# Stores of the projection results moved from the scalar engine's queue to GpSimd's

## The reference, cut to what matters

```python
(z, xbc, dt_raw, gq, gk, gv, gr, glr, mq, mk, mv, mi, mf, mo, br) = jnp.split(h @ p['w_in'], idx, axis=-1)
...
y, ssd_new = _ssd_scan(xs * dt[..., None], dt * a, bm, cm, s0)
...
o, gla_new = _gla_scan(q, k, v, la.reshape(bsz, length, GLA_HEADS, GLA_DK), gla0.astype(f32))
...
hm, (mc_new, mn_new, mm_new) = _mlstm_scan(q, k, v, ig, lf, mc0.astype(f32), mn0.astype(f32), mm0.astype(f32))
...
merged = (g[:, :, 0] * (y_a @ p['w_br_ssd']) + g[:, :, 1] * (y_b @ p['w_br_gla'])
          + g[:, :, 2] * (y_c @ p['w_br_ml']))
return merged @ p['w_out'], (conv_new, ssd_new, gla_new, mc_new, mn_new, mm_new)
```

## Time and profile before

| | us |
|---|---|
| median of 3 runs | 1900.76 |
| the 3 runs | 1897.83, 1900.76, 1903.87 |
| the profiled execution, whole | 1900.96 |
| its span (first to last instruction) | 1899.2 |
| PE busy | 1755.5 (92%) |
| DVE busy | 882.7 (46%) |
| ACT busy | 580.6 (31%) |
| POOL busy | 108.1 (6%) |

### The profile page before, as it was taken

How to read it: one execution, slowest core, us unless ns; L and a number is a source line. 1 busy time by engine, 2 the same in 40 slices (tenths; PEclk the granted TensorE clock), 3 DMA queues, 4 the chain that set the end, 5 groups by cost and what they waited for, 6 DMA issues and landing times.

```text
span 1899.2 us, 30580 instructions
## 1 busy us (share of the span) xinstructions
PE 1755.5 (92%) x12284; PEld 1641.1 (86%) x12284; DVE 882.7 (46%) x1563; ACT 580.6 (31%) x1189; POOL 108.1 (6%) x154
## 2 busy tenths in 40 slices
PE   3499999999799999999999889999899999999994
PEld 0477898898699999889988779999899999999993
DVE  1455535545375555433433334465564444344444
ACT  1233423333333333233333334332342222222221
POOL 0000001210032121000000000000000000000001
PEclk7599999999899999999999999999999999999997
DMA  7665332356434343764444865444323322222211
GB/s 271 179 230 182 91 107 91 117 159 199 153 115 156 110 145 124 247 189 132 144 129 137 264 203 178 157 142 157 111 68 101 89 67 73 84 67 89 67 45 56
DMA packets 237349, 257.34 MB, mean 136 GB/s; under 512 B 14995, under 2 KB 220491, under 8 KB 234136
## 3 DMA queue, kind: packets, MB, share of 16 engines
q1 hardware_dynamic: 208984, 226.54, 37.7%
q10 hardware_dynamic: 28224, 28.85, 4.5%
HBM read 196.73 MB, written 58.62 MB: 134 GB/s over the span
## 4 chain that ended last, share of the span: by engine, by line
issue 43%; PE 41%; DMA 3%; DVE 3%; ACT 1%; DVEq 1%; POOLq 1%; POOL 1%; ACTq 0%; SPq 0%; PEldq 0%; PEld 0%
PE pj_acc L639 6%; PE pj_acc L640 6%; PE pj_acc L641 6%; PE pj_acc L646 5%; PE pj_acc L647 4%; PE pj_acc L648 4%; PE mx L1822 2%; DMA ar_w<-in_w_ada 1%; PE mx L2571 1%; PE mx L1319 1%; PE mx L1332 1%; DMA mg_y<-ys 1%; DVE pj_lo L609 0%; DVE ss_state L1180 0%; PE mx L1389 0%
## 5 line engine op out<-in xcount | busy, mean ns | idle before, releaser
L639 PE MATMUL pj_acc<-pj_act_hi,pj_lo 128*128 128x320 f32 x1808 | 575.5, 318 | 0.8 <-issue 0.7
L641 PE MATMUL pj_acc<-pj_act_hi,pj_hi 128*128 128x320 f32 x1808 | 560.1, 310 | 0.0
L640 PE MATMUL pj_acc<-pj_act_lo,pj_hi 128*128 128x320 f32 x1808 | 560.1, 310 | 0.0
L639 PEld LDWEIGHTS pj_acc<-pj_act_hi,pj_lo 128*128 128x128 f32 x1808 | 341.3, 189 | 22.1 <-issue 21.0
L640 PEld LDWEIGHTS pj_acc<-pj_act_lo,pj_hi 128*128 128x128 f32 x1808 | 341.4, 189 | 3.9 <-issue 2.9
L641 PEld LDWEIGHTS pj_acc<-pj_act_hi,pj_hi 128*128 128x128 f32 x1808 | 340.9, 189 | 0.0
L609 DVE TENSOR_TENSOR pj_lo<-pj_raw,pj_hi 128x1024 fp32r<-128x1024 f32 (+1 forms) x196 | 242.6, 1242 | 162.6 <-ACT pj_hi L602 159.7
L602 ACT ACTIVATE pj_hi<-pj_raw 128x1024 fp32r<-128x1024 f32 (+1 forms) x196 | 205.2, 1053 | 223.1 <-PE mx L2855 116.3
L646 PE MATMUL pj_acc<-pj_lo,pj_act_hi 128*128 128x256 f32 x880 | 259.4, 295 | 12.5 <-DVE pj_act_lo L2649 4.4
L647 PE MATMUL pj_acc<-pj_hi,pj_act_lo 128*128 128x256 f32 x880 | 252.6, 287 | 0.0
L648 PE MATMUL pj_acc<-pj_hi,pj_act_hi 128*128 128x256 f32 x880 | 252.2, 287 | 0.0
(11 more groups left out here) (359 smaller groups left out, 2130.9 us busy)
## 6 DMA issues: line engine op xcount, KB each, us to landing
pj_raw<-in_w_in SPq DMA_DIRECT2D x50, 1024.0 KB, 5.6
ar_w<-in_w_ada SPq DMA_DIRECT2D x16, 1024.0 KB, 5.7
pm<-pj_tm_out ACTq DMA_DIRECT2D x100, 128.0 KB, 2.1
pj_raw<-in_w_ffn_gate SPq DMA_DIRECT2D x22, 512.0 KB, 4.0
pj_raw<-in_w_ffn_up SPq DMA_DIRECT2D x22, 512.0 KB, 5.3
pj_raw<-in_w_ffn_down SPq DMA_DIRECT2D x11, 1024.0 KB, 5.0
ada_w<-in_w_ada SPq DMA_DIRECT2D x8, 1024.0 KB, 11.6
ml_c_b<-in_state_mlstm_c SPq DMA_DIRECT2D x32, 256.0 KB, 4.3
```

Source lines behind the costliest of these rows:

```text
L639: nc.tensor.matmul(out, lo[:, k, col], ahi[:, k, tok], start=(k == 0), stop=False)
L640: nc.tensor.matmul(out, hi[:, k, col], alo[:, k, tok], start=False, stop=False)
L641: last = nc.tensor.matmul(out, hi[:, k, col], ahi[:, k, tok], start=False, stop=(k == KT - 1))
```

## The change

The function that begins the store of unit u-2 keeps its place in the plan (the entry of unit u) but is called in POOL's walk of the list and no longer in ACT's. Its waits go with it: for the bank to be read out, and for mo also for the tanh. The rings, the data, the semaphores and the DMAs' shapes are unchanged. In the changed program the lines of the copies in `act_unit` have numbers lower by 2 (690 is 688), those behind the new function higher by 2 (729 is 731, 1281 is 1283).

```diff
             self.split_hi(act, k, q)
         if u >= 1:
             self.act_late(act, u - 1)
-        if u >= 2:
-            self.act_store(act, u - 2)
...
-    def act_store(self, act, u):
+    def pool_unit(self, pool, u):
+        if u >= 2:
+            self.pool_store(pool, u - 2)
+
+    def pool_store(self, pool, u):
         n, x = self.units[u]
         c, r = self.chunks[n], self.ring[u]
         if c.how in self.CM:
-            self.evicted(act, u)
+            self.evicted(pool, u)
             dst = self.pt if c.how == "copy_cm" else self.gt
             row = c.dst + (x // 2) * P
-            act.dma_start(dst[row:row + P, (x % 2) * HALF:(x % 2 + 1) * HALF], self.cm_out[:, r % self.RING, :]
+            pool.dma_start(dst[row:row + P, (x % 2) * HALF:(x % 2 + 1) * HALF], self.cm_out[:, r % self.RING, :]
                           ).then_inc(self.cm_stored[r % self.RING], 16)
         elif c.how in self.TM:
-            self.evicted(act, u)
+            self.evicted(pool, u)
             if c.how == "bias_tm":
-                act.wait_ge(self.biased, self.nth[u] + 1)
-            act.dma_start(self.pm[x * P:(x + 1) * P, c.dst:c.dst + CW], self.tm_out[:, r % self.RING, :]
+                pool.wait_ge(self.biased, self.nth[u] + 1)
+            pool.dma_start(self.pm[x * P:(x + 1) * P, c.dst:c.dst + CW], self.tm_out[:, r % self.RING, :]
                           ).then_inc(self.tm_stored[r % self.RING], 16)
...
         def _(pool):
             for stage, x in plan:
-                if stage is not None:
+                if stage is None:
+                    proj.pool_unit(pool, x)
+                else:
```

## The result

The changed kernel takes 1906.59 us (median of 20 runs), the kernel before 1900.07 (20 runs beside them). The ratio is 1.0035, with a 95% interval of 1.0025 to 1.0044: **slower by 6.5 us**, more than the 0.3% (5.7 us) within which the prediction called a change none. It had forecast 1900 and "same".

What follows compares the result with a forecast made beforehand. PE, busy 1755.5 of 1899.2 us, was taken as the bound, so only its waits count. 1900.96 - 1.0 (first SSD tile) + 0 (all else) = 1899.96, by the median 1899.8, stated as 1900; range 1895 to 1908.

Steps and rivals of the forecast that it cites:

- first SSD tile: POOL's products of SSD tile 0 start at about 256.3, 25 us later, behind 13 z stores: -1.0 us.
- mLSTM's start: POOL's clearing of 74 semaphores, which PE awaits: 0 at 1.0 us a store, +1.5 at 2.88.
- What is given to POOL: A POOL store costs between 0.33 and 2.88 us, taken as 1.0; 196 us in 944, for which POOL has room.
- Price of a DMA, ACT's side: 196 stores of 0.326 us leave ACT's sequencer: 0 booked; at most 9.4 us of PE's waits could go.
- PE's wait at 234.5: In the first SSD tile, without POOL's products beside DVE's `pj_lo`, down from 3.62 to about 2.6 us: gain 0.99.
- The configuration: POOL's configuration instruction moves into the first SSD tile: up to 6.9 us cost nothing; the skill page's 6 us leaves 0.9.
- Last SSD tile: A store ready at 388.86 waits behind `xd` until 403.50 and lands about 406.6, before the copy at 408.12: 0, at worst +3.
- a sign of error: The prediction is wrong if ACT or DVE wait for a store's landing near 269 us; no such ACT wait expected.
- GLA and the clearing: Stores ahead of POOL's 42 GLA arguments: 0, at worst +5; ahead of semaphore clearing before mLSTM: 0, at worst +1.5.
- DVE and POOL don't collide at stores: Judges the rival that POOL's stores stretch DVE's `pj_lo` at 12 weight chunks: +10.3 us, 1910; chance 0.12.
- The slower case: Slower by more than 0.3% (5.7 us): collisions of DVE and POOL 0.12, dear DMAs at several places 0.04; chance 0.16.

Runs made afterwards that it cites:

- e_late: Kernel before plus four more power operations inside the last root of mLSTM (32-byte tile): ratio 1.0032 to the kernel before.
- e_warm_a: Changed kernel plus a power operation on a constant ahead of each of 15 waits for squares, 512-byte tile: ratio 1.0011 to the kernel before.
- e_after2: The changed kernel again, on the same chip as the runs with the 512-byte tile: ratio 1.0031 to the kernel before.
- e_tiny_rest: Kernel before, stores on ACT, plus 176 small POOL DMAs, none between mLSTM's fourth and last root (32-byte tile): ratio 1.0017 to the kernel before.
- e_tiny2: Kernel before, stores on ACT, plus 196 small POOL DMAs to scratch memory, repeated (32-byte tile): ratio 1.0038 to the kernel before.
- e_tiny_p2: Kernel before, stores on ACT, plus only the 65 small POOL DMAs after the clearing ahead of mLSTM, large tile: ratio 1.0018 to the kernel before.
- e_tiny_p1: Kernel before, stores on ACT, plus only the 131 small POOL DMAs before the clearing ahead of mLSTM, large tile: ratio 1.0001 to the kernel before.
- e_cm_last: Only the cm_out stores on POOL, plus one power operation ahead of mLSTM's last root (32-byte tile): ratio 1.0032 to the kernel before.
- e_cm: Kernel before with only the 96 cm_out stores moved to POOL, those of tm_out left on ACT: ratio 1.0022 to the kernel before.
- e_tm: Kernel before with only the 100 tm_out stores moved to POOL, those of cm_out left on ACT: ratio 1.0014 to the kernel before.
- e_tiny_a: Kernel before, stores on ACT, plus 196 small POOL DMAs to scratch memory, 512-byte tile: ratio 1.0032 to the kernel before.
- e_first: Kernel before with POOL only waiting for the first 13 z results, no DMA, so its first SSD products come later: ratio 1.0000 to the kernel before.

## Why the prediction was wrong, step by step

**The step that failed** is the list of handovers, from "first SSD tile" to "mLSTM's start", which ends in "+ 0". With the price of a store from "What is given to POOL" it asked which copies, products, GLA arguments and clearings come later. It did not ask two things. First, mLSTM's roots were left out, though the view of PE's waits that it read has the row `mg_y<-ys`, 7.6 us, ahead of all but one other; "ends with a DMA" was taken for "not POOL's", where the DMA only ends a chain from ACT's squares over POOL's root and DVE to a store and a load. Second, the price of a DMA was sought in the DMA instruction alone. It is 0.54 us, cheaper than the 1.0 taken, and still POOL loses up to 5 us, at the operation behind it. No row of before had a DMA of POOL and a root side by side, so the term had no price there; what the rows could have told is the slack of each POOL result, and the last root's is zero (`e_late`: 4.6 us of root, 4.6 us of wait). The sum also has no term for the clock, which by the estimate above goes with 4.0 of the 6.5 us.

By ratios that place is worth about 0.2% (4 us) in three comparisons: `e_warm_a` against `e_after2`, `e_tiny_rest` against `e_tiny2`, `e_tiny_p2` against `e_tiny_p1`. By the means of the same runs they are 1.7, 3.2 and 3.2 us, each give or take 1.8 to 2.1, and only the second leaves out the last root's DMAs alone: the first repairs all 15 roots, the third has the DMAs of all five mLSTM roots. `e_late` speaks for less: less the tile it is 1.0021, 4 us for 4.6 us of wait, so that the 2.2 to 2.4 us of the changed kernel would cost about 2 us. **The size of this term is thus 2 to 4 us of the 6.5.** What it costs beyond its wait may be clock; that is my reading and not shown. One comparison speaks against: `e_cm_last`, less the tile, is 1.0021, as `e_cm` is, though its wait fell from 9.7 to 8.3; the intervals of both, 0.001 wide to each side, leave room for either. **Open** is the rest, a third to two thirds of the loss (`e_warm_a` 1.0011, `e_tm` 1.0014 with no store of POOL among mLSTM's later roots). The profiles show candidates, none tested alone: the 0.4 to 0.7 us of wait that go with real stores ahead of the merge, the clearing, and the waits in GLA.

**Price of a DMA, ACT's side: right in kind.** POOL's stores, beside the earlier trace rows:

```profile
L731 POOL DMA_DIRECT2D pm<-pj_tm_out x100: 539/539/731, 215.6 to 873.6; - x100
...
DMA to landing us min/median/max: 2.0/2.7/7.3
```

The instruction's 0.54 us lies between the bounds 0.33 and 2.88; the landing is 0.6 us later in the median. That ACT without its stores gained nothing visible is seen in `e_tiny_a`, with the stores on ACT (1.0032), against `e_after2`, without (1.0031).

**First SSD tile: right but for the gain.** The products, beside the earlier trace rows:

```profile
257.90 0.54 POOL L731 DMA_DIRECT2D pm<-pj_tm_out  x1 [2.78 <-DVE pj_tm_out L744]
258.55 1.92 POOL L1283 TENSOR_TENSOR ss_xdt<-kp_x_tm,ss_sm 128x1024 f32<-128x1024 f32 x1
260.41 1.91 POOL L1287 TENSOR_TENSOR ss_xd<-kp_x_tm,ss_par 128x1024 f32<-128x1024 f32 x1
262.26 0.60 POOL L731 DMA_DIRECT2D pm<-pj_tm_out  x1
```

256.3 was forecast, 258.55 it is; the read-out that its store waits for began at 257.19 in place of 254.84, 2.35 us later. PE's wait at 234.5 fell from 3.62 to 2.79, 0.83 of the 0.99 forecast, but timed alone (`e_first`) this is worth 0.0000, plus or minus 0.0012: a microsecond of wait can't be told from none here, and the forecast's sum was built on it. The configuration costs nothing visible: it lies between the end of the DMA (258.44) and the start of the product (258.55).

The Trainium skill, page "GPSIMD Engine Reference", section 2.1 Instruction dispatch, has about 6 us for the first call behind it; at this place the trace does not show them.

**Last SSD tile: PE lost nothing, but for another reason than given.**

```profile
407.45 0.58 POOL L731 DMA_DIRECT2D pm<-pj_tm_out  x1
408.06 0.20 POOL L1294 TENSOR_SCALAR ss_sq<-ss_sq 128x2 f32<-128x2 f32 x1
413.25 0.72 POOL L1296 TENSOR_TENSOR ss_sq<-ss_sq,ss_power 128x2 f32<-128x2 f32 x1 [4.99 <-issue]
413.94 2.21 POOL L731 DMA_DIRECT2D pm<-pj_tm_out  x4
```

Four stores waited behind a gap of 4.99 us. ACT did wait for landings, which the prediction named as a sign of error, against:

```profile
413.03 0.38 ACT L686 ACTIVATE pj_tm_out<-pj_acc 128x256 f32<-128x256 f32 x1 [2.45 <-DMA pm<-pj_tm_out]
```

PE has no wait there: the second bank hid it.

**GLA and the clearing: seen, mis-sized, repaid.** In GLA the gap stands ahead of the store, not of the argument:

```profile
527.39 0.91 POOL L1645 TENSOR_TENSOR gl_ex<-gl_bc 128x256 f32<-128x256 f32 x1
532.04 1.10 POOL L731 DMA_DIRECT2D pm<-pj_tm_out  x2 [3.74 <-issue]
533.16 0.77 POOL L1644 TENSOR_TENSOR gl_ex<-gl_bc 128x256 f32<-128x256 f32 x1
```

Forecast was 0; PE waits 0.8 us at 540 us in one trace of the changed kernel and 0.2 in the other. At the clearing it waits 3.2 us in place of 2.2, forecast 0 to +1.5. With small DMAs in place of the stores the whole early part costs nothing that can be told (`e_tiny_p1`), as the waits at mLSTM's start shrink; for the real stores that is not shown.

**Rivals.** DVE and POOL don't collide at stores: `pj_lo` has the same median as in the earlier trace rows.

```profile
L609 DVE TENSOR_TENSOR pj_lo<-pj_raw,pj_hi x196: 682/1225/2508, 63.9 to 1857.4; 128x1024 fp32r<-128x1024 f32 x194, 128x512 fp32r<-128x512 f32 x2
```

The Trainium skill, page "SBUF — State Buffer", section "SBUF: two separate sides", has a DMA of GpSimd at 3.1 us in place of 0.62 beside a DVE copy that locks the shared ports. The longest DMA instruction of POOL here takes 0.73 us, and landings are 0.6 us later in the median, not the 2.5 that the prediction worked out from the page. The advice against this change was right for this kernel; its reason isn't what is seen. The slower case had 0.16 in the prediction, on mechanisms that did not occur as described. That the range, 1895 to 1908, holds the time is luck: it was drawn for other mechanisms.

## What to carry to other kernels

Before work is given to an engine with room, list every result that this engine makes and its slack, from producer to the wait of the bound engine, also across stores and loads: a wait that "ends with a DMA" may be a wait for any engine ahead of it. An engine that alternates between kinds of work may be slow at the change even when it has been idle; where a result is urgent, a call of the same operation on a constant ahead of its wait is worth a try (1.03 us of POOL here, in its idle time). And an added tile is a change of its own, which a control has to measure: 32 bytes cost 2 us here, 512 bytes did not show that cost.

## What the runs showed of the hardware

- On POOL a power operation 0.15 us behind its predecessor comes 0.23 to 4.99 us behind it in the changed kernel, where DMAs have been begun since the last one. The count does not set it: 0.24 us behind one DMA, 5.11 behind two, 1.79 behind twenty, 0.17 behind 21 with GLA operations in between (`e_tm`). A power operation of its own behind the last DMA repairs it (0.15 to 0.17). That POOL reloads code is my picture of it; the traces show only the gaps.
- A DMA behind POOL's elementwise GLA work starts 0.6 to 4.5 us late in the changed kernel, one behind the SSD products at once.
- A 32-byte tile in front of others costs 0.11% (0.01 to 0.21); the stores of a state then land about 0.76 us apart in place of 0.68.
